# Expert up weights in chunks of one matrix over eight feature tiles instead of both matrices over four

## The reference

```python
def moe_swiglu(x, w_router, w1, w3, w2):
    # 256 tokens of 1024 features; 8 experts, each with 3584 hidden features; 2 experts per token
    logits = jnp.einsum('nd,de->ne', xf, w_router)
    top_logits, top_idx = lax.top_k(logits, TOP_K)
    gates = jax.nn.softmax(top_logits, axis=-1)
    ...                                     # rows sorted by expert, in blocks of one expert each
    def expert_block(args):
        xb, e = args
        h = jax.nn.silu(xb @ w1[e]) * (xb @ w3[e])
        return h @ w2[e]
```

## Time and profile before

| | us |
|---|---|
| median of 3 runs | 3119.12 (3115.16 to 3120.99) |
| span of the profiled execution | 3116.3 |
| experts' stage in it, first to last product | 778.7 to 1863.0 |
| TensorE, busy with matmuls | 2897.2 |
| VectorE, busy | 1517.2 |
| ScalarE, busy | 1137.5 |

### The profile page before, as it was taken

How to read it: one execution, slowest core, us unless ns; L and a number is a source line. 1 busy time by engine, 2 the same in 40 slices (tenths; PEclk the granted TensorE clock), 3 DMA queues, 4 the chain that set the end, 5 groups by cost and what they waited for, 6 DMA issues and landing times.

```text
span 3116.3 us, 68244 instructions
## 1 busy us (share of the span) xinstructions
PE 2897.2 (93%) x26434; PEld 1884.3 (60%) x26434; DVE 1517.2 (49%) x4826; ACT 1137.5 (37%) x3085; POOL 0.2 (0%) x4
## 2 busy tenths in 40 slices
PE   9989999989988888888888989989999999999998
PEld 7768887857555555555545555444444444657887
DVE  5641005564666666666666664783322200454331
ACT  3121002231666666666656652262211100243210
POOL 0000000000000000000000000000000000000000
PEclk9999999989999999999999999999999999999999
DMA  5444434354799999999999980101122211211441
GB/s 219 163 179 172 149 136 161 141 225 162 255 333 330 335 331 342 329 331 329 331 321 328 326 310 29 67 15 41 68 68 81 81 68 68 94 42 61 156 148 68
DMA packets 205859, 576.08 MB, mean 185 GB/s; under 512 B 6496, under 2 KB 6624, under 8 KB 179040
## 3 DMA queue, kind: packets, MB, share of 16 engines
q1 hardware_dynamic: 205536, 571.72, 52.9%
HBM read 570.65 MB, written 1.05 MB: 183 GB/s over the span
## 4 chain that ended last, share of the span: by engine, by line
PE 59%; DMA 21%; DVE 12%; ACT 3%; issue 3%; DVEq 1%; SPq 1%; ACTq 0%
PE P L506 44%; DMA ring<-ws_moe 20%; DVE arena L1921 3%; PE P L943 3%; DVE ring L1921 2%; PE P L617 1%; PE P L697 1%; PE P L556 1%; DMA arena<-ws_moe 1%; PE P L627 1%; DVE small L1565 1%; PE P L636 1%; DVEq L1918 1%; ACT arena L1395 1%; PE P L894 1%
## 5 line engine op out<-in xcount | busy, mean ns | idle before, releaser
L506 PE MATMUL P<-arena,ring 128*128 128x256 f32 (+1 forms) x2784 | 896.3, 483 | 8.6 <-ACT arena L1194 7.9
L506 PEld LDWEIGHTS P<-arena,ring 128*128 128x128 f32 x2784 | 528.0, 190 | 368.2 <-issue 312.0
L943 PE MATMUL P<-arena 128*32 128x256 f32 x6496 | 372.8, 380 | 10.0 <-DMA arena<-ws_moe 8.8
L943 PE MATMUL P<-ring,arena 128*32 128x256 f32 x4256 | 275.1, 407 | 72.0 <-DMA ring<-ws_moe 70.7
L506 PE MATMUL P<-X_sb,ring 128*128 128x256 f32 x1504 | 334.8, 383 | 3.2 <-ACT X_sb L1173 1.6
L506 PEld LDWEIGHTS P<-X_sb,ring 128*128 128x128 f32 x1504 | 287.3, 192 | 45.8 <-issue 3.1
L943 PEld LDWEIGHTS P<-arena 128*32 128x32 f32 x6496 | 213.6, 110 | 153.1 <-DMA arena<-ws_moe 14.4
L1921 DVE COPY arena<-ring 128x256 f32 x1008 | 211.6, 287 | 142.2 <-DMA ring<-ws_moe 135.2
L1395 ACT ACTIVATE arena<-ring 128x256 f32 x672 | 215.8, 405 | 172.4 <-DMA ring<-ws_moe 158.9
L943 PEld LDWEIGHTS P<-ring,arena 128*32 128x32 f32 x4256 | 147.4, 116 | 181.9 <-DMA ring<-ws_moe 83.2
L1921 DVE COPY arena<-arena 128x256 f32 x1008 | 211.2, 286 | 77.2 <-DMA arena<-ws_moe 72.9
(11 more groups left out here) (373 smaller groups left out, 2700.0 us busy)
## 6 DMA issues: line engine op xcount, KB each, us to landing
ring<-ws_moe SPq DMA_DIRECT2D x84, 2048.0 KB, 14.5
arena<-ws_moe SPq DMA_DIRECT2D x84, 2048.0 KB, 15.9
ring<-ws_b SPq DMA_DIRECT2D x137, 1024.0 KB, 4.8
ring<-ws_a SPq DMA_DIRECT2D x67, 1024.0 KB, 4.9
cst_sb<-cst SPq DMA_DIRECT2D x1, 1664.0 KB, 10.6
X_sb<-xT SPq DMA_DIRECT2D x1, 1024.0 KB, 5.1
X_sb<-ctxT SPq DMA_DIRECT2D x1, 1024.0 KB, 4.9
out<-Y SPq DMA_DIRECT2D x2, 512.0 KB, 2.6
```

The source lines that it names most:

```text
L506: ins = nc.tensor.matmul(bank(i, n), blockap(s, b % SLOT), rhs(kk), start=kk == 0, stop=kk == k - 1)
L943: ins = nc.tensor.matmul(acc(g // 2)[BR * j:BR * (j + 1), g % 2], x[:, b * BR:(b + 1) * BR], weights_of(b), start=k == 0, stop=last and kk ...
```

## The change

An up chunk holds one matrix over all eight feature tiles: chunk `st` 0 has `w1`, chunk 1 has `w3`. Transfer `h` brings four of the eight experts, so each run in HBM is 4 KB; the bytes of a chunk and the number of transfers stay. A unit is now two feature tiles of one matrix (still 128 x 256 weights for each block), one contiguous piece of the buffer. A product moves 128 columns, into the half of the bank that belongs to the chunk's matrix, and there are two of them for each block and unit. Down chunks stay as they are.

```diff
+def by_half(ph):
+
+    return ph > 0 and PHASES[ph][1] < PK
...
+        def piece(row, ph, kk):
+
+            if by_half(ph):
+                return row.rearrange("p (k h c) -> p k h c", h=2, k=CK)[:, kk]
+            return row.rearrange("p (h k c) -> p h k c", h=2, k=CK)[:, :, kk]
...
-                to = mring[c % 2].rearrange("p (e h c) -> p e h c", e=NE, h=2)
                 for h in range(2):
-                    if i < PK:
+                    if by_half(ph):
+                        e = h * NE // 2
+                        to = mring[c % 2].rearrange("p (e c) -> p e c", e=NE)[:, e:e + NE // 2]
+                        src = ws_up[up_index(ph), st, :, e:e + NE // 2, :]
+                    elif i < PK:
...
-                        def rows_by(g, kk, weights_of):
-                            k = CK * st + kk
+                        def rows_by(g, k, at, n, weights_of, whole):
...
-                                ins = nc.tensor.matmul(acc(g // 2)[BR * j:BR * (j + 1), g % 2], x[:, b * BR:(b + 1) * BR],
-                                                       weights_of(b), start=k == 0, stop=last and kk == CK - 1)
+                                ins = nc.tensor.matmul(acc(g // 2)[BR * j:BR * (j + 1), g % 2, at:at + n], x[:, b * BR:(b + 1) * BR],
+                                                       weights_of(b), start=k == 0, stop=k == whole - 1)
...
+                        half_row = mring[c % 2].rearrange("p (e k c) -> p e k c", e=NE, k=KD)
...
+                        def unit_rows(g, kk, up_weights, both_weights):
+
+                            if not by_half(ph):
+                                k = CK * st + kk
+                                return rows_by(g, k, 0, 2 * P, both_weights, CK * PH_CHUNKS[ph])
+                            for k in (2 * kk, 2 * kk + 1):
+                                ins = rows_by(g, k, P * st, P, lambda b: up_weights(b, k), KD)
+                            return ins
...
-                                src = mring[c % 2][:, bass.ds(e, 1024)].rearrange("p (h k c) -> p h k c", h=2, k=CK)[:, :, kk]
+                                src = piece(mring[c % 2][:, bass.ds(e, 1024)], ph, kk)
```

More of the change, by code:

```diff
@@ L448, in _ @@
                     chunk_over(sp, c - 2)
-                to = mring[c % 2].rearrange("p (e h c) -> p e h c", e=NE, h=2)
                 for h in range(2):
-                    if i < PK:
+                    if by_half(ph):
[3 more added lines that the diff above has]
+                    elif i < PK:
+                        to = mring[c % 2].rearrange("p (e h c) -> p e h c", e=NE, h=2)[:, :, h]
                         src = ws_up[up_index(ph), h, :, :, st * CK * P:(st + 1) * CK * P]
                     else:
+                        to = mring[c % 2].rearrange("p (e h c) -> p e h c", e=NE, h=2)[:, :, h]
                         t = (2 * (i - PK) + h) * KE + PK * part
                         src = ws_dn[2 * KE * KD // SLOT + t // SLOT, :, :, t % SLOT * P:(t % SLOT + CK) * P]
-                    sp.dma_start(to[:, :, h], src).then_inc(sem(f"moe_w{c % 2}"), 16)
+                    sp.dma_start(to, src).then_inc(sem(f"moe_w{c % 2}"), 16)
             for n in range(SLOT0["moe"], len(SOURCE)):
@@ L948, in _ @@
                             banks_free(pe, ph - 1, 0)
+                        half_row = mring[c % 2].rearrange("p (e k c) -> p e k c", e=NE, k=KD)
                         w4 = mring[c % 2].rearrange("p (e h k c) -> p e h k c", e=NE, h=2, k=CK)
+                        def unit_rows(g, kk, up_weights, both_weights):
[5 more added lines that the diff above has]
+                            return ins
                         def fixed(kk):
                             for g in range(2):
-                                ins = rows_by(g, kk, lambda b: w4[:, b, :, kk])
+                                ins = unit_rows(g, kk, lambda b, k: half_row[:, b, k], lambda b: w4[:, b, :, kk])
                             return ins
@@ L966, in _ @@
                                     banks_free(pe, ph - 1, g // 2)
-                                ins = rows_by(g, kk, lambda b: CB[u % 3][:, min(b - NE, NDYN - 1)])
+                                ins = unit_rows(g, kk, lambda b, k: CB[u % 3][:, min(b - NE, NDYN - 1), k % 2 * P:(k % 2 + 1) * P],
+                                                lambda b: CB[u % 3][:, min(b - NE, NDYN - 1)])
                                 if last and kk == CK - 1 and g % 2:
```

## The result

The changed kernel takes 3292.43 us (median of 4 runs, 3286.16 to 3298.9), the kernel before 3117.14 beside it: ratio 1.0573, 95% interval 1.0546 to 1.06. The forecast was 3070, in a range of 3036 to 3122: wrong by its sign. The profiled execution has a span of 3295.3 us against 3116.3.

The account below looks back on a forecast made before the run. Transfers were taken to bound the experts' stage. A pair of up chunks falls from 25.6 to 23.8 us (22.2 transfers, 1.0 dry queue, 0.6 uneven landings); 27 pairs save 49 us, giving 3070 us, range 3036 to 3122.

Parts of the forecast that it names:

- I take 10.5, since the faster burst shows that issue can keep up: TensorE in up chunks: 384 matmuls take 10.5 us a chunk, between bounds of 10.4 and 11.0, hidden under 11.1 of transfer.
- some 4 us ... inside the range: Instruction queue: 20,736 more TensorE instructions are 1.3 MB over the same engines, some 4 us in the whole stage.
- The bursts on which the step rested: Short rows of the old trace: 48 matmuls of 64 columns at 28.7 ns each, 46 at 14 ns.
- The third rival: TensorE in up chunks: issue or weight loads hold 54.4 ns a matmul, 459 us added, 3578 us; chance 0.10.
- The transfers: Up-chunk loads: 4 KB runs cut a chunk's transfer from 12.7 to 11.1 us, a pair from 25.4 to 22.2.
- The line through 2 KB and 8 KB runs: Price of a run in the loads: 25 ns plus 36 ns a KB, giving 4 KB runs 169 ns, 387 GB/s per full share.
- dry spells: Load queue in up chunks: SP's issue comes too late, so the queue runs dry about 1.0 us per pair.
- uneven landings: Loads of up chunks: an allowance of another 0.6 us per pair.
- TensorE's rate: Up-chunk products: 128-column matmuls on four 32-column tiles come every 27.2 ns, 10.4 us a chunk, nothing added.
- No wait is added: Up chunks: both transfers still needed per chunk, fixed experts' work ends at mid-chunk, banks freed at the same places; no time added.
- the copies, for which no change was taken: Copies on VectorE and ScalarE in up chunks: count, width and order stay, no gain taken.
- The rule on runs: Loads: the Trainium skill's line rate from 512 B would make 2 KB and 4 KB runs equal; the prediction went against it.

Follow-up runs that it names:

- e7: Kernel before with 4 KB runs for up and down chunks by reordering the weights on the host, products still 256 columns: 3009.64 us, ratio 0.9613.
- e4: Kernel before with 4 KB runs for all 56 up chunks by reordering the weights on the host, products still 256 columns: 3041.5 us, ratio 0.9753.
- e2: Kernel before with its 2 KB runs, each up-chunk product after the first phase split in two of 128 columns: 3367.21 us, ratio 1.0799.
- e6: Changed kernel, each up-chunk transfer after the first phase brings 128 KB instead of 2 MB, same instructions: 3077.32 us, ratio 0.983.
- e1: Changed kernel, up-chunk products after the first phase move 64 of their 128 columns, same instruction count: 3276.14 us, ratio 1.0507.

## Why the prediction was wrong

**The step that failed** is in TensorE's part: "I take 10.5, since the faster burst shows that issue can keep up", and the instruction queue's "some 4 us ... inside the range". The bytes were right (1.33 MB more, 1.3 forecast), but bytes are not what the queue costs. The supply is a round trip for each 256 instructions, and the question was whether 256 are used up sooner than the next come. The bursts on which the step rested have 46 and 48 matmuls, with their weight loads 92 and 96 instructions: less than half a block, so they could not show it. Before, a block lasts 128 x 54.4 ns = 7.0 us, and the median gap at its end was under 0.01 us; after, it lasts 3.5, and 130 of the stage's 211 gaps are over 0.15 us, 253 us in all from start to start (218.8 in the waits, which begin where the last matmul ends). Of the trace of before, the packets' size and count were on the page: 16 KB each, which against instructions of the same page gives the block and its 7 us. The round trip beside the loads was there in part, in single packets of the trace: for the 112 blocks of before's stage that meet a share over 0.9, the instruction packet begins 3.2 us (median) after the block's start and has ended by 4.1, later than the 3.5 us that a block of the changed kernel lasts. What could not be read is the 1.4 us from there to TensorE's next instruction (last section), since no block was used up fast enough to show it.

**The third rival was the right one, at another price.** It named instruction supply, put the decision at 32 ns a matmul and the time at 3578. The stage's 179 us over 27 pairs make 6.6 a pair: 32.2 us, less 0.8 for the flips, over 768 matmuls is 41 ns. So it decided where it said, but the spacing is not fixed at 54 ns: it is 27 where a block is not waited for, and (3.4 + 2.6) / 128 = 47 ns beside loads. Its chance of 0.10 leaned on the short bursts.

**The transfers** were right or better. Packets are 150,644 (150,600 forecast). The line through 2 KB and 8 KB runs gave 387 GB/s per full share; e7, whose stage has only 4 KB runs, has 359 / 0.93 = 386. In after's short full stretches (the DMA view above) most slices have 393 to 431. The 49 us forecast for the up chunks were too few: e4, which has this part alone, gained 77 with 28 pairs, 2.75 a pair where 1.8 were forecast and 3.4 without dry spells, so the 1.6 us a pair for dry spells and uneven landings was too much. Beside the split they are worth 75 us too (e2 against the change), but not as forecast: TensorE sets the pace there, and the profiles differ by 43 us in its waits for issue (261.3 and 218.8), 27 in its busy time (2978.0 and 2950.9) and 6 in its waits for loads (25.7 and 20.2).

**TensorE's rate** of 27.2 ns a matmul between block ends was right (27.1). The Trainium skill ("TensorE: Matmul & The Clock Gate", section "Back-to-back issue gap") would have had 81 ns; the rows of after disagree for these tiles.

**"No wait is added"** did not hold, and the copies, for which no change was taken, came late. No wait was written into the code, but a stall of TensorE holds its products, these hold the copies (146.4 us of idle time in one group), the copies SP's issue, and the loads that would follow: the DMA row above reads 0 in its first seven slices, 5 us. The dry spells looked for came from this, not from faster transfers.

**The rule on runs.** The Trainium skill ("DMA: Bandwidth & Descriptors", section "Specifications") has line rate from 512 B on. e4 and e7 disagree: the same bytes in 4 KB runs take 77 and 120 us less. Another rule of the Trainium skill bears on the failed step: "Runtime: NRT & Kernel Launch", section "Instruction fetch mechanics", says that an engine's instructions come in blocks of 16 KiB by a DMA queue of its own while the block before is executed, at a cost that is mostly hidden. The traces agree on the block (256.0 instructions to a packet), and before agrees that it is hidden (under 0.01 us); after does not (2.60 us a block beside loads).

## What to carry to other kernels

Before splitting instructions on an engine that runs beside saturated transfers, work out how long 256 of them last and compare it with the round trip of the instruction queue, here 3.6 us with free engines, 6.0 beside 4 KB runs and 6.7 beside 2 KB runs; a burst shorter than a block proves nothing. Waits of "issue" with no releaser, at equal counts of instructions, are its mark in a profile. If a longer run in memory is what is wanted, get it from the order of the data, not from more and smaller instructions.

## What the runs showed of the hardware

- TensorE's instructions arrive in packets of 16 KB for 256 of them. At a stall it resumes 1.4 us (median) after the end of such a packet, which itself takes 1.0 us. With the engines nearly free (e6, share under 0.2) the packet begins 1.1 us (median) after TensorE has started on the block before; in after, at shares over 0.8, 3.7. With the engines free that makes 3.6 us from block to block, a round trip that just about fits 128 small matmuls (3.4). A stock of several blocks does not show: the first stall of after's stage, 1.75 us, ends the second block that is used up fast (it starts at 815.5 us), though the three blocks before the two took 6.9, 16.9 and 6.7 us without a gap. When a block is asked for, no run shows.
- Beside 2 KB runs the gap is longer than beside 4 KB runs: 3.30 us (67 blocks of e2) against 2.60 (77 of after), at shares over 0.8. Whether the instruction packet queues behind the load's packets in each engine was not tried.
- The granted clock is lower where TensorE stalls more. It goes to and fro between its two levels, 1.2 and 2.4 GHz, and its mean share is 0.83 in e1 and 0.94 in after (both 820 to 2030 us; 381.4 and 218.8 us of issue waits), and 0.99 in e7's stage (2.8 us).
